# Retention chunks: another order of products, swapped outputs, and the heads' normalisation on ScalarE

## The reference, cut to what matters

```python
h = rmsnorm(x, g_pre)
proj = h @ w_in                                  # 1024 x 6144: q, k (8 heads of 128), v, gate (8 of 256)
q = rope(q, pos); k = rope(k, pos) * 128 ** -0.5
# per head, chunks of 64 tokens: decayed scores inside, a running state R across
scores = einsum(q, k) * inner_dec;  inner = scores @ v
cross = (q @ R) * xi;  R = R * g_c + (k * zeta).T @ v
o = inner + cross
o = (o - mean(o)) * rsqrt(var(o) + 1e-6) * gn_gain        # over each head's 256 values
y = (silu(gate) * o) @ w_out
x = x + rmsnorm(y, g_post)
```

## Time and profile before

| | us |
|---|---|
| median of three runs | 2488.24 (2488.09 to 2489.24) |
| the profiled execution | 2486.97 |
| its span, first to last instruction | 2485.2 |
| PE busy | 2388.8 (96%) |
| DVE busy | 1639.2 (66%) |
| ACT busy | 1045.8 (42%) |
| POOL busy | 817.5 (33%) |

### The profile page before, as it was taken

The page is one execution under the profiler, slowest core; times in us unless marked ns, Lnnn a source line. Parts: engine busy times, 40 slices in busy tenths (PEclk is TensorE's granted clock), DMA queues, the critical chain, the costliest instruction groups (busy, mean ns, idle before and its releaser), DMA issues.

```text
span 2485.2 us, 33132 instructions
## 1 busy us (share of the span) xinstructions
PE 2388.8 (96%) x11720; PEld 2008.7 (81%) x11720; DVE 1639.2 (66%) x2666; ACT 1045.8 (42%) x1902; POOL 817.5 (33%) x732
## 2 busy tenths in 40 slices
PE   6879999899999999999999999999999999999998
PEld 5667787787788898888888888888888888888887
DVE  6657898787631441177775686787548766787785
ACT  6335444544621342355554444454334332333332
POOL 5365665575422230532221010011124333333112
PEclk9989999999999999999999999999999999999999
DMA  5444344343753513122234311111433434563422
GB/s 205 111 128 136 124 137 127 123 141 107 262 173 120 161 52 106 53 58 62 62 117 160 106 33 56 46 47 64 135 109 129 161 132 178 222 241 138 170 93 85
DMA packets 157307, 302.69 MB, mean 122 GB/s; under 512 B 13729, under 2 KB 83489, under 8 KB 155681
## 3 DMA queue, kind: packets, MB, share of 16 engines
q1 hardware_dynamic: 157152, 300.71, 36.0%
HBM read 207.33 MB, written 89.13 MB: 119 GB/s over the span
## 4 chain that ended last, share of the span: by engine, by line
PE 74%; DVE 10%; issue 5%; ACT 4%; POOL 4%; DMA 2%; SPq 0%; DVEq 0%; ACTq 0%; POOLq 0%
PE ff_ps L4322 11%; PE ff_ps L4349 10%; PE wa_y_ps L516 7%; PE gl_vr_ps L2953 7%; PE ra_even_ps L1540 4%; PE wb_y_ps L3310 4%; PE gl_j_ps L2912 4%; PE la_x_ps L1747 4%; PE ra_apart_ps L1540 3%; PE wc_y_ps L3691 3%; PE ff_ps L4380 2%; PE la_cq_ps L1686 1%; PE la_kv_ps L1686 1%; DVE ra_w_lower L1285 1%; DVE ra_sTl L1326 1%
## 5 line engine op out<-in xcount | busy, mean ns | idle before, releaser
L4349 PE MATMUL ff_ps<-ff_p,ff_p 128*128 128x512 f32 x1176 | 268.1, 390 | 0.3 <-DVE ff_odd L4209 0.3
L4349 PEld LDWEIGHTS ff_ps<-ff_p,ff_p 128*128 128x128 f32 x1176 | 220.3, 188 | 48.1 <-issue 1.8
L2680 POOL TENSOR_SCALAR gl_mo<-gl_so 128x1 f32<-128x1 f32 x32 | 16.0, 501 | 333.0 <-ACT gl_osq L2618 333.0
L3968 ACT ACTIVATE ff_p<-ff_h 128x1024 fp32r<-128x1024 f32 x51 | 54.1, 1061 | 163.0 <-PE ff_ps L4349 163.0
L1285 DVE TENSOR_TENSOR ra_w_lower<-ra_b,ra_w_upper 128x1024 fp32r<-128x1024 f32 x60 | 92.5, 1542 | 34.8 <-ACT ra_w_upper L885 34.5
L4193 DVE TENSOR_TENSOR ff_p<-ff_h,ff_p 128x1024 fp32r<-128x1024 f32 x51 | 80.7, 1582 | 42.7 <-ACT ff_p L3968 42.7
L516 PE MATMUL wa_y_ps<-wa_wh,wa_gl 128*128 128x512 f32 x256 | 103.4, 404 | 4.2 <-ACT ra_c L901 4.2
L1540 PE MATMUL ra_even_ps<-ra_s_upper,ra_w_lower 128*128 128x512 f32 x264 | 104.0, 394 | 1.1 <-DVE ra_s_lower L1279 1.0
L1540 PE MATMUL ra_even_ps<-ra_s_lower,ra_w_upper 128*128 128x512 f32 x264 | 103.4, 392 | 0.0
L1540 PE MATMUL ra_even_ps<-ra_s_upper,ra_w_upper 128*128 128x512 f32 x264 | 103.1, 391 | 0.0
L2953 PE MATMUL gl_vr_ps<-gl_vrh,x_lower 128*128 128x512 f32 x256 | 102.1, 399 | 0.0
(11 more groups left out here) (579 smaller groups left out, 7617.6 us busy)
## 6 DMA issues: line engine op xcount, KB each, us to landing
ff_h<-hidden SPq DMA_DIRECT2D x53, 512.0 KB, 3.3
ra_b<-in_w_chunks_a SPq DMA_DIRECT2D x48, 512.0 KB, 4.4
staging<-heads_a SPq DMA_DIRECT2D x64, 256.0 KB, 2.9
hidden<-ff_s SPq DMA_DIRECT2D x29, 512.0 KB, 2.8
ff_v<-in_w_ff SPq DMA_DIRECT2D x28, 512.0 KB, 6.8
ff_b<-in_w_ff SPq DMA_DIRECT2D x24, 512.0 KB, 5.6
hidden<-ff_a SPq DMA_DIRECT2D x24, 512.0 KB, 2.7
gated_a<-ra_oS SPq DMA_DIRECT2D x64, 128.0 KB, 1.9
```

Source lines behind the costliest of these rows:

```text
L4349: end = pe.matmul(to[:, u, :], a[:, k, i * P:(i + 1) * P], b[:, k, :], start=(opens and p < 3 and k == 0 and m == 0), stop=(k == 1 and m = ...
```

## The change

What it does, part by part:

- A head's v becomes the first columns of its chunk, q and k the last: v is now C11 and C21, q and k are C12 and C22. What is rotated and what is stored plain change places.
- The products' order is 0, 1, 2, 3, 4, 6, 5 for the first two chunks and 0, 1, 3, 4, 2, 6, 5 from then on. C22 is now copy of 4 plus product 2; the weight sums come in the order T1, T2, T3, T4, with the sign of T2 and of the sum s2 turned.
- The opening: ScalarE runs a one-column activation first; the first weight block is loaded and split in halves; x's blocks aren't scaled by ScalarE (except x22), the gains go into VectorE's instructions (`weigh`, `rows_lower`) in pieces; x's rows have four buffers and tiles 4 to 7 are squared first; scales, tables and stores stand in another order in SyncE's queue; the second token half of q and k is rotated first.
- The tiles start four slots later, and each step after the scores one slot later. `normalize` is an activation on ScalarE, o * rstd + shift; GpSimd makes shift = -mean * rstd as a third operation of `deviation`.
- Around the end: rows of the output weights have other places and wait for other products, gate stores and loads another order, and the last tile starts with other rows.

```diff
-    heads = np.concatenate([q[:, :, 0], k[:, :, 0], q[:, :, 1], k[:, :, 1], v], axis=2).reshape(DM, -1)
+    heads = np.concatenate([v, q[:, :, 0], k[:, :, 0], q[:, :, 1], k[:, :, 1]], axis=2).reshape(DM, -1)
...
+        ORDERS = ((0, 1, 2, 3, 4, 6, 5), (0, 1, 3, 4, 2, 6, 5))
...
-        OPENING, CLOSING = 2 * SLOTS + 4, CHUNKS * SLOTS - 4
+        OPENING, CLOSING = 2 * SLOTS + 8, CHUNKS * SLOTS - 4
...
-        ATTEND, DEVIATE, NORM, STORE = 2, 3, 5, 6
+        ATTEND, DEVIATE, NORM, STORE = 3, 4, 6, 7
...
@@ SyncE
+            def load_very_first():
+                src = w_chunks[0, B11, :, :].rearrange("p (k n) -> p k n", k=KT // 2)
+                for half in range(2):
+                    at = slice(2 * half, 2 * half + 2)
+                    sp.dma_start(raws[0][B11][:, at, :], src[:, at, :]).then_inc(x11_in[0] if half == 0 else raw_in[0][B11], 16)
...
-            load_rows(4)
-            load_rows(5)
-            load_rows(6)
-            load_rows(7)
-            store_values(0, 1)
+            for t in range(4, NT):
+                load_rows(t)
+            store_values(0, 0)
+            store_values(1, 0)
+            load_scale(1)
...
             load_raw(2, B12)
+            load_scale_row(1)
             load_scale(0)
+            load_raw(2, B22)
             load_scale_row(0)
-            load_scale_row(1)
-            store_values(1, 1)
             load_raw(2, B21)
-            store_turned(1, 0)
-            load_raw(2, B22)
-            store_turned(0, 0)
-            store_values(0, 0)
             store_turned(1, 1)
             store_turned(0, 1)
-            store_values(1, 0)
+            store_turned(1, 0)
+            store_values(0, 1)
+            store_values(1, 1)
+            store_turned(0, 0)
...
-                    if c < FINAL and slot in (1, 3, 7, 9):
-                        load_raw(c + 1, {1: B11, 3: B12, 7: B21, 9: B22}[slot])
+                    if c < FINAL and slot in (1, 6, 8, 10):
+                        load_raw(c + 1, {1: B11, 6: B12, 8: B22, 10: B21}[slot])
...
@@ ScalarE
+            def normalize(h, t):
+                act.wait_ge(rstd_done, h * NT + t + 1)
+                act.activation(oS[:, t % 4, :], oS[:, t % 4, :], ACT.Identity, scale=rstd[:, t, 1:2], bias=shift[:, t:t + 1]).then_inc(G_done, 1)
...
                 if at := tile_at(c, slot, ATTEND):
                     attend_step(*at)
+                if at := tile_at(c, slot, NORM):
+                    normalize(*at)
...
+            act.wait_ge(neghalf_set, 1)
+            act.activation(warm[:, :], neghalf[:], ACT.Copy)
             act.wait_ge(gains_in, 16)
-            rows_upper(x11, a11, x11_in, 0)
-            w_upper(0)
+            for half in range(2):
+                act.wait_ge(x11_in[half], (32, 16)[half])
+                rows_upper(x11, a11, 0, (2 * half, 2 * half + 2))
+                first_upper(half)
...
@@ GpSimd
             def deviation(h, t):
...
-                pool.wait_ge(rstd_part, s + 1)
-                pool.tensor_tensor(rstd[:, t, 1:2], rstd[:, t, 0:1], neghalf[:], ALU.pow).then_inc(rstd_done, 1)
+                pool.wait_ge(rstd_part, 2 * s + 1)
+                pool.tensor_tensor(rstd[:, t, 1:2], rstd[:, t, 0:1], neghalf[:], ALU.pow).then_inc(rstd_part, 1)
+                pool.wait_ge(rstd_part, 2 * s + 2)
+                pool.tensor_scalar(shift[:, t:t + 1], mv[:, t, 0:1], rstd[:, t, 1:2], -1.0, ALU.mult, ALU.mult).then_inc(rstd_done, 1)
...
                     if slot == 0 and c < CHUNKS:
+                        sum_of(c, T3)
+                    if slot == 1 and c - 1 in GATE_CHUNKS:
+                        scale_gates(c - 1, 3)
+                    if slot == 2 and c < CHUNKS:
                         sum_of(c, T4)
...
-                        if slot == 4:
-                            scale_gates(c, 0) if head is None else rotate(head, 0)
-                        if slot == 6 and c < FINAL:
+                        if slot == 4 and head is None:
+                            scale_gates(c, 0)
+                        if slot == 8 and c < FINAL:
                             sum_of(c + 1, T1)
-                        if slot == 10 and head is None:
-                            scale_gates(c, 1)
+                        if slot == 10:
+                            scale_gates(c, 1) if head is None else rotate(head, 1)
                         if slot == 11 and c < FINAL:
-                            sum_of(c + 1, T3)
                             sum_of(c + 1, T2)
                         if slot == 12:
-                            scale_gates(c, 2) if head is None else rotate(head, 1)
+                            scale_gates(c, 2) if head is None else rotate(head, 0)
...
@@ VectorE
-            def normalize(h, t):
-                s = h * NT + t
-                dve.wait_ge(rstd_done, s + 1)
-                dve.tensor_scalar(oS[:, t % 4, :], oS[:, t % 4, :], mv[:, t, 0:1], rstd[:, t, 1:2],
-                                  ALU.subtract, ALU.mult).then_inc(G_done, 1)
...
                 if n == 1:
-                    dve.wait_ge(xg_done, 2)
+                    dve.wait_ge(x21_in, 16)
                     dve.tensor_tensor(s3_sum, x11[:, :, :], x21[:, :, :], ALU.subtract).then_inc(xs_done, 1)
-                    form_lower(s3, s3_sum, 9)
                 if n == 2:
-                    form_lower(a22, x22[:, :, :], 10)
+                    rows_lower(s3_sum, s3, 8, 0, (0, 4))
                 if n == 3:
...
+                    for half in range(2):
+                        dve.wait_ge(xg_done, half + 1)
+                        weigh(x21, x21, 0, x22, ALU.add, half)
+                    for half in range(2):
+                        dve.wait_ge(xs_done, half + 2)
+                        weigh(x11, x11, 0, x21, ALU.subtract, half)
```

## The result

| | before | after |
|---|---|---|
| median, us | 2488.7 (four runs) | 2449.6 (2448.7 to 2452.6, four runs) |
| profiled execution | 2486.97 | 2450.13 |
| half product 36, where the first scores now stand | 156.1 (worked out in the prediction) | 131.1 |
| from there to the end of the chunks | 497.8 | 478.9 |
| from there to the end of the execution | 1833.1 | 1840.1 |

The ratio is 0.9837, with a 95% interval of 0.9814 to 0.9860: 39 us faster, where 66 were forecast. The direction was right, and so were some of the mechanisms; the time lies 29 us above the forecast and just outside its range. The end of the chunks is where the output product first waits or starts, 653.9 us before and 610.0 after.

The account below looks back on a forecast made before the run. TensorE was taken as the bound, with idle and half-clock time to win: -37 opening, -12.6 order, -9 and +4 normalisation, -5 half clock, -6.5 end, -66 from 2486.97 to 2421 us; range 2404 to 2448.

Parts of the forecast that it names:

- First matmul: Start of the opening: split first weight block and early table load end product 0 at 17.0 for 20.5 us, -3.5.
- Preparing x: Opening: gains move into VectorE's instructions, the first addition comes before its bank is wanted, 3.7 us wait left; net -4.5.
- Scales and rotation: Opening: scale row near 64 us, rotations end near 103, first tile there near 114, first scores at 119 us.
- rival C: Opening stays tied to the rotation: first tile lands some 12 us after TensorE wants it; 2438 us, chance 0.09.
- forecast 117.4 us: Opening: when TensorE reaches the first scores by its work and waits, before 2 us added for a lower part.
- Opening as a whole: All up to the first scores, first matmul and x included: 119 us for 156.1, -37, bounds -30 and -42.
- Order of products: Middle: each addition gets a whole product of cover, so 11 waits for additions go; -12.6, or 0 if cover fails.
- Normalisation and later slot: Middle: normalisation leaves VectorE, tile steps a slot later; -9 of 14.0 us of waits, +4 for waiting on GpSimd's scale.
- Rival D: Middle, six rotating chunks: ScalarE held by a tile's scale behind two rotations, 12 us each; 2493 us, chance 0.05.
- Half clock in the middle: Middle: four half-clock stretches of 3.4 us cost 6.8 us and mostly go with their waits; -5 (0 to -6.8).
- End of the chunks: End: last copies come before a step waiting for gates, so a 4.2 us wait and half-clock loss go; -6.5.
- Rival B: Middle isn't freed, waits reappear at other places; only opening and end gain; 2443 us, chance 0.16.

Follow-up runs that it names:

- sums_after: Changed kernel with GpSimd's T2 sums of the first two chunks held until VectorE has made x's lower part for the third product; 2451.5 us, ratio 0.9850.
- after_opening: Changed kernel with the first scores four half products earlier, at half product 32 as in the kernel before; 2466.3 us, ratio 0.9895.
- late_sp: Changed kernel with VectorE's second odd rotation behind the lower parts, its store behind those of values and even rotation in SyncE's queue; 2447.2 us, ratio 0.9832.
- before_opening: Kernel before with only the first tile's scores four half products later, at half product 36; 2494.2 us, ratio 0.9999.
- norm_back: Changed kernel with the normalisation back on VectorE and no bias on GpSimd; 2465.7 us, ratio 0.9911.
- opening_only: Changed kernel with the middle's three parts undone (order of products, normalisation, later slots); 2481.0 us, ratio 0.9968.
- rows_first: Changed kernel with ScalarE making a weight row's upper part ahead of that of a product of gates in the same slot; 2443.0 us, ratio 0.9820.
- combined: Changed kernel with late_sp, rows_first, sums_after, first chunks' additions ahead of x's pieces, and the last gate scaling and finish later; 2439.1 us, ratio 0.9798.

## Why the prediction was right and wrong

The miss of 29 us divides by stage: the first scores at 131.1 us where 119 were forecast (+12.1), the middle 478.9 where 497.8 - 22.6 = 475.2 were (+3.7), the rest 1840.1 where 1833.1 - 6.5 = 1826.6 were (+13.5).

- *First matmul*: the end of product 0 came as forecast, at 16.9 us for 17.0, but not by the way that was argued. The first matmul came at 9.1 us where 7.5 was estimated, and the product then ran without a wait between its halves, where it was to wait for the second half of x; so the hit is in part luck.
- *Preparing x* (-4.5): mis-sized. A wait of 3.7 us and 1.5 of half clock were left standing at the sixth product; it was 6.3 at the fifth, with 6.8 us at half clock in which TensorE was busy 4.7, so 2.4 lost: a cost of 8.7 us for the old pair's 9.7, a gain of 1.0. The step that failed: the first addition was to come before TensorE wants the bank, since the pieces of x were taken as if alone on VectorE. They were nearly twice as long beside GpSimd's sums (9.09 us for 4.87 in sums_after). Even alone they left no gain, as VectorE's next pieces were then waited for.
- *Scales and rotation*: the scale path was moved ahead as argued, but it and the rotations were late too. The first scale row, forecast at 64 us, was spread from 66.9 and landed 8.3 us later, at 75.3; the rotations ran from 85.6 to 112.1 us, where 80 to 103 was forecast; the first tile's load was issued at 121.2 and landed 4.6 us later, at 125.8, where 114 was forecast. It wasn't waited for only because TensorE itself came later, at 131.1. That is luck, not a point for the argument: rival C's condition, a tile that lands after TensorE wants it, held against the forecast 117.4 us (8.4 us late, where C had 12), and the wait shows where TensorE is earlier (4.7 us in after_opening, 2.7 in late_sp). The term that failed for the time itself is the 2 us for the lower part behind VectorE's second odd rotation: 8.0 us, and 2.0 more of half clock. The mechanism and the place were named; the rotation took from 100.88 to 112.1 us beside one on GpSimd, and it was priced from a rotation of GpSimd's alone, not as VectorE's queue.
- *Opening as a whole* (-37): 25 at the first scores. That the opening's gain passes through the middle whole, as the sum takes it by adding the two, failed too: 9.6 us gained there left nothing in before_opening, and 6.6 left 2.7 in late_sp. The premise ahead of the sum, that the chunks' gain arrives whole, failed by 7 us: 43.9 us were gained at the end of the chunks, 36.8 in the execution.
- *Order of products* (-12.6): the additions' waits went whole, and alone the order is worth 12.1 us, in the changed kernel 8. For product 4, which needs the copy of 3, the step "no row shows a wait there, so nothing" failed: that copy in the new order waits for stores, 5.4 us.
- *Normalisation and later slot* (-9 and +4): right in sign, far too small; 19.3 us together, neither worth much without the other. Rival D is out: ScalarE did wait 17.3 us for GpSimd's bias, and its norm_back is slower, not faster.
- *Half clock in the middle* (-5): none was left of the four stretches, so the 6.8 us came whole.
- *Not in the sum*: some 11.2 us by which the rest of the change lengthens the middle (opening_only). It and the undersized normalisation nearly cancel, so the middle's total came out close (+3.7) by two errors: luck again.
- *End of the chunks* (-6.5): the 4.2 us wait went as argued, and with it, as I read it, the time in which ScalarE and VectorE got ahead of TensorE. The step that failed is that nothing was asked to be late next: the chain of rows and products, 5.1 us, a weight row, 2.9 us, and 10.2 us at half clock, which cost some 3.7. rows_first gives 6.6 us back.

Rival B's mechanism (waits reappear at other places) is what happened at the opening and the end, and in the middle, where it was placed, only in part: 5.4 us of copies came for 12.6 of additions that went.

## What to carry to other kernels

When a wait in front of the bounding engine goes, look up what its helpers did in that time: here most removed waits showed the next one, at VectorE, SyncE's queue, a store or GpSimd, and only rows_first (6.6 us by the medians) and combined (10 us) made the changed kernel clearly faster. Price each small step of a helper as it runs beside the others, not alone. Parts of a change that share an engine can be worth something together that none is worth alone (here 19.3 us), so undo them in pairs as well as one by one.

## What the runs showed of the hardware

In this kernel small instructions of VectorE with both inputs in SBUF, started beside a long one of GpSimd, end just behind it; those with one input in PSUM take their usual time. VectorE's and GpSimd's timelines of the changed kernel:

```profile
404.46 1.96 DVE L1377 TENSOR_TENSOR ra_ql<-staging,ra_qh 128x128 fp32r<-128x128 f32 x1 [1.03 <-ACT ra_qh L951]
406.35 0.34 DVE L1380 SCALAR_TENSOR_TENSOR ra_kzl<-ra_T_ps,ra_zr,ra_kzh 128x128 fp32r<-128x128 f32 x1
406.61 0.41 DVE L1382 TENSOR_TENSOR ra_vl<-ra_T_ps,ra_vh 128x256 fp32r<-128x256 f32 x1
406.94 1.90 DVE L1384 TENSOR_TENSOR ra_sTl<-ra_sT,ra_sTh 128x128 fp32r<-128x128 f32 x1
```

```profile
403.88 2.40 POOL L1169 TENSOR_TENSOR ra_b<-ra_b,ra_b 128x1024 f32<-128x1024 f32 x1
406.23 2.46 POOL L1188 TENSOR_TENSOR ra_c<-ra_c,ra_rms_row 128x1024 f32<-128x1024 f32 x1
```

The first and the last piece (both inputs in SBUF; the last takes 0.28 us at 215.44 us, where GpSimd is idle) end at 406.42 and 408.84 us, 0.14 and 0.15 behind the ends of GpSimd's sum (406.28) and scaling (408.69); the two between them, with ra_T_ps in PSUM, take 0.34 and 0.41 beside it. Over the whole middle it is the same: the 64 instructions of L1377 and of L1384 took 0.27 to 2.5 us each, those of L1380 0.34 to 0.35 and of L1382 0.40 to 0.43. The Trainium skill (SBUF — State Buffer, section Who interferes with whom) says that an instruction of VectorE with two SBUF inputs contends with one of GpSimd that reads SBUF. The trace agrees by the numbers above, and the opening's pieces of x, 9.09 us and 4.87 when the sums are moved, are where it bore on this change, though shortening them alone gained no time.
